# One step of a hybrid mLSTM, pooling and expert layer: latent attention through a carried state, with the masks on GpSimd

## The reference

```
b = cumsum(fc)                                   # log of the forget gates
dmat = where(lower, b[t] - b[s] + ic[s], NEG)    # weights inside a chunk
m_t = max(b + m, max_s dmat)
s = (q @ k.T) * exp(dmat - m_t)
num = exp(b + m - m_t) * (q @ C) + s @ v
den = exp(b + m - m_t) * (q @ n) + sum(s)
h = num / max(|den|, exp(-m_t))
C_new = decay * C + (w_state * k).T @ v          # state carried to the next chunk
n_new = decay * n + sum(w_state * k)
```

## Time and profile before

| What | Value |
|---|---|
| Median of three runs | 1079.4 us (1077.72 to 1080.03) |
| Profiled execution | 1075.08 us, its span 1073.3 us |
| PE busy | 993.5 us (93%) |
| PE weight loads busy | 873.2 us (81%) |
| DVE busy | 634.5 us (59%) |
| ACT busy | 515.3 us (48%) |
| POOL busy | 133.7 us (12%) |
| Chain that ended last, by engine | PE 84%, DVE 6%, DMA 5%, ACT 2% |
| Transfer of `nm` / `wib`, median from issue to landing | 7.0 / 6.1 us |

### The profile page before, as it was taken

One profiled execution on the slowest core, in us unless ns is written; L12 is line 12 of the kernel. 1 busy time (PEld: TensorE's weight loads), 2 busy tenths in 40 slices (PEclk: granted clock), 3 DMA queues, 4 the chain that ended last, 5 costly groups with the idle time before them and its releaser, 6 DMA issues.

```text
span 1073.3 us, 14490 instructions
## 1 busy us (share of the span) xinstructions
PE 993.5 (93%) x5934; PEld 873.2 (81%) x5934; DVE 634.5 (59%) x774; ACT 515.3 (48%) x656; POOL 133.7 (12%) x135
## 2 busy tenths in 40 slices
PE   6899999999999999999999999982999999999970
PEld 2378888899888989999998998882788888888860
DVE  0645643323476768232116444536699999999987
ACT  2353343413556664222214123223578787878763
POOL 3000000000110100896000000001011111111010
PEclk9899999999999999999999999985899999999995
DMA  9734434421334324231221124521899999999955
GB/s 348 312 118 176 176 135 184 157 105 40 89 93 119 92 57 156 107 126 66 79 79 67 56 75 182 229 94 64 360 379 416 422 411 417 413 419 416 396 231 203
DMA packets 36066, 216.41 MB, mean 202 GB/s; under 512 B 4352, under 2 KB 4800, under 8 KB 15520
## 3 DMA queue, kind: packets, MB, share of 16 engines
q1 hardware_dynamic: 27024, 180.23, 43.2%
q0 software_dynamic: 8112, 32.53, 8.7%
q10 hardware_dynamic: 864, 2.73, 0.6%
HBM read 200.68 MB, written 14.79 MB: 201 GB/s over the span
## 4 chain that ended last, share of the span: by engine, by line
PE 84%; DVE 6%; DMA 5%; ACT 2%; issue 1%; SPq 0%; DVEq 0%; POOL 0%; ACTq 0%; POOLq 0%
PE ps L1476 81%; DMA rowA<-yscr 2%; DMA raw<-in_wst 1%; PE ps L1857 1%; DVE xr L1454 1%; DVE rowB L1451 1%; DVE hn L958 1%; PE ps L1875 1%; DMA xg<-h2scr,slot_rows 1%; DVE hlo L971 0%; DVE hn L976 0%; DVE xr L1458 0%; PE ps L1808 0%; DMA yscr<-yb,slot_rows 0%; PE ps L1740 0%
## 5 line engine op out<-in xcount | busy, mean ns | idle before, releaser
L932 DVE TENSOR_TENSOR wlo<-raw,whi 128x2048 fp32r<-128x2048 f32 x37 | 86.1, 2329 | 146.9 <-ACT whi L579 146.9
L1476 PE MATMUL ps<-hhi,whi 128*128 128x320 f32 x672 | 153.9, 310 | 1.7 <-ACT gF L616 1.7
L1476 PE MATMUL ps<-hlo,whi 128*128 128x320 f32 x672 | 153.1, 309 | 0.0
L1476 PE MATMUL ps<-hhi,wlo 128*128 128x320 f32 x672 | 153.0, 309 | 0.0
L1476 PEld LDWEIGHTS ps<-hhi,whi 128*128 128x128 f32 x672 | 112.6, 188 | 4.9 <-ACT gF L616 2.0
L1476 PEld LDWEIGHTS ps<-hhi,wlo 128*128 128x128 f32 x672 | 112.4, 188 | 0.0
L1476 PEld LDWEIGHTS ps<-hlo,whi 128*128 128x128 f32 x672 | 112.4, 188 | 0.0
L579 ACT ACTIVATE whi<-raw 128x2048 fp32r<-128x2048 f32 x37 | 70.5, 1907 | 85.9 <-PE ps L1476 83.7
L1351 DVE TENSOR_TENSOR wlo<-raw,whi 128x2048 fp32r<-128x2048 f32 x32 | 72.6, 2289 | 5.4 <-ACT whi L859 5.3
L1351 DVE TENSOR_TENSOR olo<-raw,ohi 128x2048 fp32r<-128x2048 f32 x32 | 72.5, 2288 | 4.5 <-ACT ohi L859 4.5
L859 ACT ACTIVATE whi<-raw 128x2048 fp32r<-128x2048 f32 x32 | 61.3, 1919 | 18.3 <-PE ps L1476 18.3
(11 more groups left out here) (331 smaller groups left out, 2253.1 us busy)
## 6 DMA issues: line engine op xcount, KB each, us to landing
raw<-in_wexp SPq DMA_DIRECT2D x64, 1024.0 KB, 8.8
raw<-in_wst SPq DMA_DIRECT2D x60, 1024.0 KB, 5.0
eraw<-in_wexp SPq DMA_DIRECT2D x32, 1024.0 KB, 7.5
nm<-negscr POOLq DMA_DIRECT2D x8, 640.0 KB, 7.0
wib<-wiscr POOLq DMA_DIRECT2D x8, 512.0 KB, 6.1
xT<-in_x SPq DMA_DIRECT2D x4, 640.0 KB, 10.8
xr<-in_xt SPq DMA_DIRECT2D x1, 2560.0 KB, 10.9
h2scr<-ht ACTq DMA_DIRECT2D x5, 512.0 KB, 3.0
```

Of the source, the lines that this page charges most:

```text
L932: dve.tensor_tensor(lo[:, :], raw[s][:, :], f32(hi[:, :]), ALU.subtract)\
L1476: return nc.tensor.matmul(out, lhsT, rhs, start=start, stop=stop)
```

## The change

The latent tokens become four chunks of 128 that pass a state on. Per head:

- PE computes only the five diagonal score blocks (`score(h, 0)` four latent ones, `score(h, 2)` the context's), transposes the keys of all five tiles, and in the new `states(h)` multiplies the transposed, weighted keys `kw` of three tiles per direction with the values: six products with 129 columns.
- DVE, in the new `chunk_states(h)`, adds these up in three steps of two instructions: each state `cs` is the one before it times a decay, plus the product in PSUM. The decays are two small copies out of `wib`.
- `values(h)` computes a tile and direction from one state and one diagonal block. Its PSUM banks are fixed now; tile 2 goes to bank 4 and tile 3 to bank 5, where the products of `states(h + 1)` lie until `chunk_states(h + 1)` has read them, so tile 2 waits for `s_cs` of head h + 1.
- `off_exps` and the products with `OFF` are gone; `S` is double-buffered; `mask_maxima` runs on GpSimd, in its list behind `load_maxima(h + 1)` and ahead of `load_inter(h)`; `wib` has one buffer, and the scaled queries go to `qd`.
- Once, ahead of the heads, eight small DVE instructions on 16 rows prepare the chunk ends, and four more transposes the state weights.

```diff
...
             def load_inter(h):
-                if h >= 2:
-                    gp.wait_ge(s_pv, 6 * h - 6)
-                gp.dma_start(wib[h % 2][:, :, :], wiscr.rearrange("(d h) t -> h d t", h=H)[h, :, :]
-                             .partition_broadcast(P)).then_inc(d_wib[h % 2], 16)
+                if h:
+                    gp.wait_ge(s_qd, h)
+                gp.dma_start(wib[:, :, :], wiscr.rearrange("(d h) t -> h d t", h=H)[h, :, :]
+                             .partition_broadcast(P)).then_inc(d_wib, 16)
+
+            def mask_maxima(h):
+                gp.wait_ge(d_nm[h % 2], 16 * (h // 2 + 1))
+                if h:
+                    gp.wait_ge(s_exp, 2 * h)
+                for d in range(2):
+                    neg = cst[:, (C_NEGF, C_NEGB)[d]:(C_NEGF, C_NEGB)[d] + P]
+                    gp.tensor_tensor(nmd[:, d, :].rearrange("p (t n) -> p t n", n=P),
+                                     nm[h % 2][:, d, :].rearrange("p (t n) -> p t n", n=P),
+                                     neg.unsqueeze(1).broadcast_to([P, NT, P]), ALU.add)\
+                      .then_inc(s_mask, 1)
 
...
-            for h in range(2, H):
-                load_maxima(h)
+            for h in range(1, H):
+                if h < H - 1:
+                    load_maxima(h + 1)
+                mask_maxima(h)
                 load_inter(h)
             gp.wait_ge(st_free, H)
...
             def score_out(h, i):
-                n = 5 * h + i
+                n = 3 * h + i
                 act.wait_ge(s_sc, n + 1)
                 if i == 0:
...
+                        for x in range(3):
+                            t, r = CHAIN[d][x], h + d * H
+                            ins = act.activation(kw[d][:, x, :], ps[:, n % 2, (t - 1) * P:t * P],
+                                                 ACT.Copy, scale=ws_tok[:, t, r:r + 1])
                 else:
...
+                    act.activation(S[h % 2][:, 0, :], ps[:, n % 2, 0:P], ACT.Copy)
+                    for d in range(2):
+                        r = h + d * H
+                        ins = act.activation(kc[h % 2][d][:, :], ps[:, n % 2, P:2 * P], ACT.Copy,
+                                             scale=ws_tok[:, 0, r:r + 1])
...
                 if h < H - 1:
-                    act.wait_ge(s_p, h + 1)
+                    if h:
+                        act.wait_ge(s_p, h)
                     score_out(h + 1, 0)
                     diag_exps(h + 1, 0)
+                    act.wait_ge(s_dc, h + 1)
                     score_out(h + 1, 1)
                     diag_exps(h + 1, 1)
                     score_out(h + 1, 2)
-                    off_exps(h + 1, 0)
-                    off_exps(h + 1, 1)
-                    score_out(h + 1, 3)
-                    score_out(h + 1, 4)
                     gate_out(h + 1)
                     gate_hi(h + 3)
...
             def scale_queries(h):
-                dve.wait_ge(d_wib[h % 2], 16 * (h // 2 + 1))
-                dve.tensor_tensor(wib[h % 2][:, :, :], wib[h % 2][:, :, :],
+                dve.wait_ge(d_wib, 16 * (h + 1))
+                if h >= 2:
+                    dve.wait_ge(s_pv, 6 * h - 6)
+                for d, a in ((0, P - 1), (1, P)):
+                    st.on(dve.tensor_copy(dec[h % 2][:, d, :], wib[:, d, a:a + 3 * P - 1:P]))
+                dve.tensor_tensor(qd[h % 2][:, :, :], wib[:, :, :],
                                   by(QK[:, h, TC:T].unsqueeze(1), [P, 2, TL]), ALU.mult)\
                    .then_inc(s_qd, 1)
 
+            def chunk_states(h):
+                dve.wait_ge(s_dc, h + 1)
+                st.wait()
+                for x in range(3):
+                    for d in range(2):
+                        t = x if d == 0 else 2 - x
+                        prev = cs[h % 2][:, d, x - 1, :] if x else stC[:, d, h, :]
+                        ins = dve.scalar_tensor_tensor(
+                            cs[h % 2][:, d, x, :], prev, dec[h % 2][:, d, t:t + 1],
+                            ps[:, 4 + d, x * V1:(x + 1) * V1], ALU.mult, ALU.add)
+                        if x == 2 and d == 1:
+                            ins.then_inc(s_cs, 1)
+                        else:
+                            st.on(ins)
+                    if x < 2:
+                        st.wait()
+
             def products(h):
-                dg, off = DG[h % 2], OFF[h % 2]
-                dve.wait_ge(s_sev, 5 * h + 5)
+                dve.wait_ge(s_sev, 3 * h + 3)
                 for d in range(2):
                     dve.wait_ge(s_exp, 2 * h + d + 1)
...
+                    ins = dve.tensor_tensor(DG[h % 2][d][:, :, :], DG[h % 2][d][:, :, :],
+                                            S[h % 2][:, :, :], ALU.mult)
                 ins.then_inc(s_p, 1)
...
             products(0)
             scale_queries(0)
+            chunk_states(0)
             gate_lo(2)
-            mask_maxima(1)
             for h in range(H):
                 if h < H - 1:
                     scale_queries(h + 1)
-                if h < H - 2:
-                    mask_maxima(h + 2)
-                if h < H - 1:
                     products(h + 1)
                     gate_lo(h + 3)
+                    chunk_states(h + 1)
                 for t in range(NT):
                     head_rows(h, t)
...
             def score(h, i):
-                n = 5 * h + i
+                n = 3 * h + i
                 if n >= 2:
                     pe.wait_ge(s_sev, n - 1)
                 q, k = QK[:, h, :], QK[:, H + h, :]
...
+                for x, t in enumerate(range(1, NT) if i < 2 else (0, 0)):
+                    out, kt = ps[:, n % 2, x * P:(x + 1) * P], k[:, t * P:(t + 1) * P]
+                    if i == 0 or (i == 2 and x == 0):
+                        last = mm(out, kt, q[:, t * P:(t + 1) * P], True, True)
+                    else:
+                        last = nc.tensor.transpose(out, kt, ident)
                 last.then_inc(s_sc, 1)
...
+            def states(h):
+                pe.wait_ge(s_sev, 3 * h + 2)
+                if h:
+                    pe.wait_ge(s_cs, h)
+                if h >= 2:
+                    pe.wait_ge(pv_free, NT * (h - 1) - 1)
+                for d in range(2):
+                    for x in range(3):
+                        last = mm(ps[:, 4 + d, x * V1:(x + 1) * V1], kw[d][:, x, :],
+                                  Vt[:, CHAIN[d][x], h, :], True, True)
+                last.then_inc(s_dc, 1)
 
             def values(h):
                 hp = h % 2
                 pe.wait_ge(s_p, h + 1)
                 for t in range(NT):
-                    bank = bank_of(6 * h + t)
+                    if t == 0 and h:
+                        pe.wait_ge(pv_free, h * NT)
+                    elif t == 1 and h:
+                        pe.wait_ge(st_free, h)
+                    elif t == 2 and h < H - 1:
+                        pe.wait_ge(s_cs, h + 2)
+                    elif t == 4:
+                        pe.wait_ge(pv_free, h * NT + 1)
                     if t == 1:
                         pe.wait_ge(s_qd, h + 1)
+                        pe.wait_ge(s_cs, h + 1)
                     for d in range(2):
-                        out = ps[:, bank, d * V1:(d + 1) * V1]
...
+                        out = ps[:, VAL_BANK[t], d * V1:(d + 1) * V1]
                         if t:
-                            mm(out, wib[hp][:, d, (t - 1) * P:t * P], stC[:, d, h, :], True, False)
-                        for s in tiles:
-                            if s == t:
-                                w = DG[hp][d][:, t, :]
-                            elif d == 0:
-                                o = OFF_F[s - 1] + (t - s - 1) * P
-                                w = OFF[hp][0][:, o:o + P]
-                            else:
-                                o = OFF_B[s - 2] + (t - 1) * P
-                                w = OFF[hp][1][:, o:o + P]
-                            last = mm(out, w, Vt[:, s, h, :], t == 0, s == tiles[-1])
+                            x = t - 1 if d == 0 else NL - t
+                            state = cs[hp][:, d, x - 1, :] if x else stC[:, d, h, :]
+                            mm(out, qd[hp][:, d, (t - 1) * P:t * P], state, True, False)
+                        last = mm(out, DG[hp][d][:, t, :], Vt[:, t, h, :], t == 0, True)
                     last.then_inc(s_pv, 1)
...
             for h in range(H):
                 if h < H - 1:
                     score(h + 1, 0)
+                    gate_quarter(h + 1, 0, 0)
                     score(h + 1, 1)
-                    gate_quarter(h + 1, 0, 0)
+                    gate_quarter(h + 1, 0, 1)
                     score(h + 1, 2)
-                    gate_quarter(h + 1, 0, 1)
-                    score(h + 1, 3)
                     gate_quarter(h + 1, 1, 0)
-                    score(h + 1, 4)
+                    states(h + 1)
                     gate_quarter(h + 1, 1, 1)
                 values(h)
...
```

(32 more changed lines are left out.)

102 lines of the change are left out of this document (38 added, 64 removed).

## The result

| | Before | Changed kernel |
|---|---|---|
| Median | 1078.56 us (4 runs, 1075.04 to 1080.03) | 1088.7 us (4 runs, 1087.28 to 1092.79) |
| Ratio of the changed kernel to the one before | | 1.0103, 95% interval 1.0076 to 1.013 |
| Profiled execution, its span | 1075.08, 1073.3 us | 1088.49, 1086.7 us |
| PE busy | 993.5 us (93%) | 976.1 us (90%) |
| First matmul behind the heads | 416.83 | 425.88 |

The changed kernel is 1.0% slower. PE does 17 us less and the span is 13 us longer. Of this, 9.05 us have arisen by the end of the heads, and another 1.1, which I did not trace, by PE's last products of the experts (1035.51 before, 1045.69 after). The last 3.3 us come from the last scatter of the experts, which took POOL 5.33 us to issue in the changed kernel and 2.03 before.

A forecast was written before the change was run, and what follows sets the result against it. PE bound the kernel before; after, a path over ACT and DVE would set the round. +0.5 us for the path and +5.2 for the clock made +5.7 on the median of 1079.4: 1085.1 us, range 1078.0 to 1091.0.

The forecast's parts named there:

- The path: From PE's last gate quarter over ACT and DVE back to PE at tile 2: rounds of 18.3 us, +0.5 in all.
- the clock: PE's granted clock falls in half of the seven waits, 1.5 us each: +5.2 us, ends 0 and 15.8.
- round 0: First round of the heads: as long as the others; wib's delay by masks, between 0 and 3 us, taken as 0.
- the opening: Opening scores and states(0), ahead of the rounds: -2.1 + 1.3 = -0.8 us, so round 0 begins at 280.1.
- PE's own round of 14.5 us: PE's work in one round of the heads after the change: 14.5 us against 18.0 before.
- The end of the stage: PE waits in round 7 for DVE's rows of head 6; heads end at 417.0, +0.2 us, or +0.5 with rounding.
- The masks on GpSimd: Adding the masks on GpSimd takes 3.1 to 4.9 us a head, beside other work: costs nothing.
- rival 2: GpSimd's masks and DVE's products exclude each other, so gate_lo starts 0.8 us later a round: 1085.5 us, chance 0.10.
- Rival 4: States are ready when PE reaches tile 2, rounds are PE's 14.5 us: about 1057 us, chance 0.05.

The follow-up runs named there:

- both last experiments: Changed kernel with gate_lo behind all rows, and masks on DVE between row tiles (1055.3 us) or later on GpSimd, behind the products and wib's DMA (1054.27 us).
- The first experiment: Changed kernel with chunk_states(h+1) moved ahead of gate_lo(h+3) in DVE's list: 1074.05 us, 0.9964 of the kernel before.
- the filled wait: Changed kernel with 15 unread products of 129 columns put into each of PE's seven waits for the states: 1082.21 us, ratio 1.0031 to the kernel before.
- the last kernel: Changed kernel with gate_lo behind all rows, masks on GpSimd waiting for the products and issued after wib's DMA: 1054.27 us, ratio 0.9776 to the kernel before.

## Why the prediction was right

It said slower, 1085.1 us in a range of 1078.0 to 1091.0; the time is 1088.7. As a change it said +5.7 and +10.1 came. The path and the kind of its costs are borne out, while three terms, the clock, round 0 and the opening, all came out too small, one of them by the spread of one execution. By its steps:

- **PE's own round of 14.5 us** is right: 14.50 where nothing else binds (both last experiments).
- **The path** is right, term by term: 0.20 from the last quarter to `gate_out`, 0.7 to `gate_hi` (312.35, 313.04 on ACT's timeline), 1.1 to `gate_lo`, 1.14 to the states, 1.95 from there to PE, where 0.2, 0.7, 1.1, 1.1 and 2.0 stood. Round 18.32, predicted 18.3. The wait of 3.8 us that I had is one of 3.56 in the trace, and 0.26 beyond it. The first experiment shows that `gate_lo` ahead of the states is the cause, with 15 us from one swap, and with `gate_lo` behind the rows too, 24 come back.
- **The clock** was the right mechanism with too small a size. Five waits lost it, where I had booked three and a half; a fall takes 1.65 us, not 1.5; and the last one is made up by a shorter wait in `values(7)`. That leaves 4 x 1.65 = 6.6 us, and the filled wait gives 6.5 from the medians (although it loses 0.6 of its own in `values(7)`), where 5.2 stood. Half of the waits was a guess that came near: no run says why it is five of seven here.
- **The opening** was to start round 0 at 280.1; it starts at 281.11, 0.2 behind the 280.93 of before. PE's part of it is right, 10.56 us from the first score to round 0 (270.55 to 281.11), against 11.19 before. But the first score came at 270.55, and in the six experiments, where PE's list up to there is the same, at 269.63 to 270.09, and round 0 at 280.19 to 280.65. So most of the 1.0 is the spread of this one execution.
- **Round 0** I left at the length of the others, with `wib` "between 0 and 3 us" taken as 0. Without its fall it takes 21.00 - 1.65 = 19.35 us, 1.0 more. 0.3 are a later first gate quarter: it starts 1.14 us into the round (282.25), behind the end of `gate_out(0)` at 282.11, and in round 1 0.81 (302.92). 0.7 are `gate_out`, which may not start before `scale_queries` is through, and that is late twice: its `wib` comes late, since GpSimd issues that DMA only behind the first masks, and then it runs beside the second masks (two rows of DVE's timeline):

```profile
289.50 0.28 DVE L1104 COPY dec<-wib 128x3 f32<-128x3 f32 x2 [5.19 <-DMA wib<-wiscr]
289.69 2.60 DVE L1105 TENSOR_TENSOR qd<-wib,QK 128x1024 f32<-128x1024 f32 x1
```

It takes 2.60 us where 1.22 is usual, and ACT starts at 292.38. The run with the masks on DVE shows that the masks on GpSimd are the cause: its round 0 is 0.7 shorter, as given above. It does not part the late `wib` from the slower scaling.
- **The end of the stage** came at 425.88. From my 417.3 without any clock: +1.0 start, +1.0 round 0, +6.6 clock, and -0.2 since the other six rounds were 18.32 and not 18.36. That is 425.7, and 0.2 are left over.
- **The masks on GpSimd** I priced at nothing. Six rounds of seven bear that out, round 0 does not (0.7 us), but the contention is larger than I allowed: rival 2 was to decide from 2.1 us a mask on, and a mask takes 1.54 alone and 1.83 beside the products, while the products go from 1.56 to 3.78 for two. They had 1.1 us of room left.
- **Rival 4**, that the gain arrives, was put at 1057 us, "only if `gate_lo` did not wait for `gate_hi`". With `gate_lo` out of the way it was 1064.3, and 1054 to 1055 with the masks moved too.

The Trainium skill bears on two of these. On the masks, the trace of the changed kernel shows 1.55 us alone (round 0) and 3.78 beside POOL for two products with both inputs in SBUF, the on-chip memory, and no change for `cs`, which reads one input from PSUM, where matmuls leave their results. The skill's page "GPSIMD Engine Reference", section "Key points", says that GpSimd shares its SBUF interfaces with VectorE and gets in the way of instructions with two SBUF inputs. The trace agrees as to these kinds of instruction; the section gives no size. On the clock, five of seven waits of 3.55 to 4.26 us lost it. By the skill's page "TensorE: Matmul & The Clock Gate", section "HAM oscillation — how this bites in real kernels", all seven would have lost it. At 1.65 us each that is an estimate of 11.6 us. The trace does not agree, and the measurement decides.

## What to carry to other kernels

When work is taken off the engine that binds, follow the loop once around through the other engines, from its last instruction to the first that waits for them: that path may be the new bound. Ahead of the instruction that releases the binding engine, put nothing in the list that waits for a third engine; one line moved was worth 15 us here, and moved to the right place 24. And count with a wait twice: a TensorE that waits 3.6 us may pay another 1.65 us at half clock when it resumes, so that idle products in the wait can even be a gain.

## What the runs showed of the hardware that I had not expected

- The price of a fall lies almost wholly on work. In the changed kernel the clock fell 0.4 to 1.3 us after PE had resumed, in all five cases. The earliest elsewhere was 0.3 us before that, in `values(7)` of the run with the states ahead (404.04, PE back at 404.35) and of the one with the masks on DVE between the rows (385.70, 385.96).
- The length of a wait does not decide whether the clock is lost. Waits of 3.55 us at the same place of the list lost it in four rounds of six and held it in two, and which these are differs between kernels of the same rhythm. In `values(7)` shorter waits did the same: it was lost behind 2.87 us in the run with the filled wait and behind 2.41 and 2.42 in the last two kernels, and held behind 2.87 with the masks on DVE and behind 2.42 with `gate_lo` last. What tells them apart stays open.
- Two DVE products of 128x640 with both inputs in SBUF take 1.56 us alone and 3.78 beside two such sums on GpSimd, which themselves go from 3.08 to 3.66. DVE alone does the two products and the two masks in 3.03 us. Split over two engines, and met at the same time, the same work keeps DVE busy for longer than that. The second product ends 0.7 us behind the second mask, about one product later, as if it had not run beside it at all.
- The waiting can fall on DVE alone. The scaling of the queries in round 0 went from 1.22 to 2.60 us beside the second of two masks that kept their 3.08. In round 0 of the run with `gate_lo` last, two copies of 128x3, 0.23 us elsewhere, took 1.64 beside the masks and ended with them (290.45 and 290.42).
- The instructions of `cs`, with one input in PSUM, were not slowed at all (1.25 us for four, beside POOL and alone), nor were the rows that met the masks in the last kernel (`HO` 0.35 us as before).
